# A decoder layer's start: modulation summed by one-column products, x transposed into SBUF, first loads in another order

## What is computed

```python
mod = silu(c) @ w_ada + b_ada                 # w_ada (1024, 3072)
shift, scale, gate = split(mod, 3)
h = x * rsqrt(mean(x*x) + eps) * norm_gain * (1 + scale) + shift
proj = h @ w_in                               # w_in (1024, 4808), split into u_a z_a q k v z_b q_idx k_idx w_idx g_a g_b
y_a = pooling(u_a) * silu(z_a)
y_b = sparse_attention(q, k, v, top 256 keys by the index scores of q_idx, k_idx, w_idx) * silu(z_b)
out = x + gate * ((sigmoid(g_a) * (y_a @ w_branch_a) + sigmoid(g_b) * (y_b @ w_branch_b)) @ w_out)
```

## Time and profile before

| | us |
|---|---|
| median of 3 runs | 896.79 |
| lowest, highest | 895.34, 902.83 |
| span of the profiled execution (first to last instruction) | 892.1 |

### The profile page before, as it was taken

The page is one execution under the profiler, slowest core; times in us unless marked ns, Lnnn a source line. Parts: engine busy times, 40 slices in busy tenths (PEclk is TensorE's granted clock), DMA queues, the critical chain, the costliest instruction groups (busy, mean ns, idle before and its releaser), DMA issues.

```text
span 892.1 us, 13967 instructions
## 1 busy us (share of the span) xinstructions
PE 805.7 (90%) x4991; PEld 710.8 (80%) x4994; DVE 623.8 (70%) x1238; ACT 338.3 (38%) x602; POOL 358.0 (40%) x301
## 2 busy tenths in 40 slices
PE   0349999998999999999999878899999999989998
PEld 0348999988988888887788756688888787869998
DVE  6974022787878898898888845577778895774542
ACT  4525322365562122223232112566667662320100
POOL 6414462055632577862652211654423002781110
PEclk9999999999999999999999979999999999999999
DMA  9811121113211331231123311633312005946432
GB/s 346 287 40 38 48 70 36 38 51 104 84 48 48 95 95 48 94 105 37 47 84 96 104 45 61 204 105 107 107 48 72 12 2 157 330 137 205 140 96 72
DMA packets 65200, 87.96 MB, mean 99 GB/s; under 512 B 5706, under 2 KB 44142, under 8 KB 65136
## 3 DMA queue, kind: packets, MB, share of 16 engines
q1 hardware_dynamic: 35116, 38.86, 14.2%
q10 hardware_dynamic: 28100, 41.96, 14.0%
q0 software_dynamic: 1920, 6.29, 1.9%
HBM read 66.12 MB, written 20.97 MB: 98 GB/s over the span
## 4 chain that ended last, share of the span: by engine, by line
PE 49%; DVE 35%; issue 5%; DVEq 5%; ACT 4%; DMA 1%; ACTq 0%; SPq 0%
DVE junk L1677 19%; PE pp L504 11%; PE pp L506 11%; PE pp L505 11%; PE pp L794 3%; PE ps L623 3%; PE ps L622 3%; PE pt L777 3%; DVE accept L1689 3%; DVE ada_acc L1520 2%; DVE cand L1691 2%; DVEq L1793 1%; PE pt L805 1%; DVE pT L1740 1%; DVE m_raw L1808 1%
## 5 line engine op out<-in xcount | busy, mean ns | idle before, releaser
L461 POOL TENSOR_TENSOR w_lo<-w_raw,w_hi 128x1024 fp32r<-128x1024 f32 (+1 forms) x54 | 131.9, 2461 | 201.4 <-ACT w_hi L450 201.1
L1677 DVE TENSOR_SCALAR_CACHE_REDUCE junk<-score,cand 128x384 uint8<-128x384 f32 (+1 forms) x186 | 168.6, 944 | 19.3 <-issue 13.3
L504 PE MATMUL pp<-hT_hi,w_hi 128*128 128x512 f32 x384 | 151.2, 394 | 0.0
L506 PE MATMUL pp<-hT_hi,w_lo 128*128 128x512 f32 x384 | 150.3, 391 | 0.0
L505 PE MATMUL pp<-hT_lo,w_hi 128*128 128x512 f32 x384 | 150.2, 391 | 0.0
L504 PE MATMUL pp<-w_hi,hT_hi 128*128 128x256 f32 (+1 forms) x416 | 119.2, 286 | 0.6 <-POOL hT_lo L1282 0.6
L506 PE MATMUL pp<-w_hi,hT_lo 128*128 128x256 f32 (+1 forms) x416 | 117.4, 282 | 0.0
L505 PE MATMUL pp<-w_lo,hT_hi 128*128 128x256 f32 (+1 forms) x416 | 117.3, 282 | 0.0
L504 PEld LDWEIGHTS pp<-hT_hi,w_hi 128*128 128x128 f32 x384 | 72.7, 189 | 16.1 <-issue 0.8
L506 PEld LDWEIGHTS pp<-hT_hi,w_lo 128*128 128x128 f32 x384 | 72.5, 189 | 15.3
L505 PEld LDWEIGHTS pp<-hT_lo,w_hi 128*128 128x128 f32 x384 | 72.6, 189 | 14.9
(11 more groups left out here) (246 smaller groups left out, 1737.1 us busy)
## 6 DMA issues: line engine op xcount, KB each, us to landing
w_raw<-in_w_in SPq DMA_DIRECT2D x36, 512.0 KB, 3.7
ada_w<-in_w_ada SPq DMA_DIRECT2D x8, 1024.0 KB, 14.4
sgb_spill<-stage ACTq DMA_DIRECT2D x16, 256.0 KB, 2.0
sga_spill<-stage ACTq DMA_DIRECT2D x16, 256.0 KB, 2.0
stage<-sga_spill ACTq DMA_DIRECT2D x16, 256.0 KB, 2.7
ma_spill<-stage POOLq DMA_DIRECT2D x16, 256.0 KB, 2.4
e_in<-sgb_spill ACTq DMA_DIRECT2D x16, 256.0 KB, 5.0
e_in<-ma_spill ACTq DMA_DIRECT2D x16, 256.0 KB, 6.4
```

The source lines that it names most:

```text
L461: nc.gpsimd.tensor_tensor(w_lo[:, ci % 2, 4 * p:4 * p + 4, 0:width], w_raw[:, n % RAW, :, 0:width], w_hi[:, ci % 2, 4 * p:4 * p + 4, 0:wid ...
L504: nc.tensor.matmul(o, a_hi, b_hi, start=first, stop=False)
L506: return nc.tensor.matmul(o, a_lo, b_hi, start=False, stop=last)
L1677: v.tensor_scalar(junk[:, n % 2, 0:keys(b)], score[:, score_at(b):score_at(b + 1)], least, None, ALU.is_ge, ALU.add, accum_out=cnt[:, n:n ...
```

## The change

- w_ada is loaded as seven row blocks ada_w[:, k, 0:2048] (1 MB, 8 KB per partition) for k = 0..6, then weight piece 0, then block 7 in two halves, piece 1, x tiles 0 and 1, piece 2 (which waits for the first w_lo), x tiles 2 and 3, wg_raw, the other pieces.
- The modulation is made on TensorE: for k = 1, 3, 5, 6, 7 (ADA_PE) 16 one-column products ada_w[:, k, ch]^T times c_silu[:, k], each into a column of its own in PSUM. k = 0, 2, 4 (ADA_V) are weighted and summed on VectorE in three 2048-column steps (ada_acc), then 16 products against ones. VectorE reduces the 6 x 16 columns. GpSimd does nothing for it.
- The transposes of half 1 are copied from PSUM to a new SBUF tile xT and stand between the column products in TensorE's program; h is made in place in xT once the modulation is known.
- Tiles 0 and 1 are made together, k by k, in both PSUM banks. hT_lo of half 1 is VectorE's for k in HT_V, GpSimd's for 5 and 7.
- GpSimd splits both pieces of chunk 0 as before; ScalarE's second hi split now comes after hT_hi of k = 1. Squares, root, scaling and transposes of half 0 move behind tiles 0 to 4 and 5 to 7 (H_AFTER), and `ps_value` counts one use of ps for the modulation instead of four.

```diff
-        return ps_at[key] + 4
+        return ps_at[key] + 1
-            lambda s: alloc(s, "ada_w", [P, 4, KD, HALF]),
+            lambda s: alloc(s, "ada_w", [P, KD, 2 * D]),
-            return alloc(s, "x_in", [P, NT, D]), alloc(s, "ada_acc", [P, 4, HALF])
+            return (alloc(s, "x_in", [P, NT, D]), alloc(s, "xT", [P, KD, HALF]), alloc(s, "ada_acc", [P, 2 * D]))
+        ADA_PE, ADA_V = [1, 3, 5, 6, KD - 1], [0, 2, 4]
+        ADA_COLS = 2 * D // P
+        HT_V, HT_P = [0, 1, 2, 3, 4, 6], [5, 7]
...
@@ sync @@
-            for i in range(4):
-                for j in range(2):
-                    ks = slice(j * KD // 2, (j + 1) * KD // 2)
-                    sp.dma_start(ada_w[:, i, ks], ada[:, ks, i * HALF:(i + 1) * HALF]).then_inc(ada_in[2 * i + j], 16)
-            for t in range(NT // 2):
-                sp.dma_start(x_in[:, t, :], x[t * P:(t + 1) * P, :]).then_inc(x_tile_in[t], 16)
+            for k in range(KD - 1):
+                sp.dma_start(ada_w[:, k, :], ada[:, k, 0:2 * D]).then_inc(ada_in[k], 16)
+            load_piece(0)
+            sp.dma_start(ada_w[:, KD - 1, 0:D], ada[:, KD - 1, 0:D]).then_inc(ada_in[KD - 1], 16)
+            sp.dma_start(ada_w[:, KD - 1, D:2 * D], ada[:, KD - 1, D:2 * D]).then_inc(ada_end, 16)
+            load_piece(1)
+            load_x(0)
+            load_x(1)
+            load_piece(2)
+            load_x(2)
+            load_x(3)
...
-        H_AFTER = {n: KD + 2 * (n - 1) for n in range(1, 5)}
+        H_AFTER = {5: [KD, KD + 1], 6: [KD + 2, KD + 3, KD + 4], 7: [KD + 5, KD + 6, KD + 7]}
@@ tensor @@
+            modulation = ps_claim("ada")
+            def ada_columns(i, first=0, end=ADA_COLS):
+                k = ADA_PE[i] if i < len(ADA_PE) else None
+                for j in range(first, end):
+                    ch, to = slice(j * P, (j + 1) * P), modulation[:, i * ADA_COLS + j:i * ADA_COLS + j + 1]
+                    if k is None:
+                        nc.tensor.matmul(to, ada_acc[:, ch], ones[:, 0:1], start=True, stop=True)
+                    else:
+                        last = nc.tensor.matmul(to, ada_w[:, k, ch], c_silu[:, k:k + 1], start=True, stop=True)
+                return last if k is not None else None
+            pe.wait_ge(c_silu_done, 1)
+            for i in range(2):
+                pe.wait_ge(ada_in[ADA_PE[i]], 16)
+                ada_columns(i)
             for n in range(2):
                 h_transposes(n)
...
+            pe.wait_ge(ada_in[ADA_PE[2]], 16)
+            ada_columns(2)
+            for n in range(2, 5):
+                h_transposes(n)
+            pe.wait_ge(ada_in[ADA_PE[3]], 16)
+            ada_columns(3)
+            for n in range(5, KD):
+                h_transposes(n)
+            pe.wait_ge(ada_sum, 1)
+            ada_columns(len(ADA_PE))
+            pe.wait_ge(ada_in[KD - 1], 16)
+            ada_columns(4, 0, ADA_COLS // 2)
+            pe.wait_ge(ada_end, 16)
+            ada_columns(4, ADA_COLS // 2).then_inc(ps_full, 1)
...
+            early = [pp_claim(("qi", i, t)) for i, t in QI_ORDER[:2]]
+            for k in range(KD):
+                if k % 4 == 0:
+                    pe.wait_ge(w_lo_done, k // 4 + 1)
+                pe.wait_ge(hT_hi_done, k + 1)
...
+                for o, (i, t) in zip(early, QI_ORDER):
+                    last = rows_step(o, t, name_of[("qi", i)], k, CW)
+                    if k == KD - 1:
+                        last.then_inc(pp_full, 1)
...
                 if n == NT:
                     pe.wait_ge(hT_hi_done, 2 * KD)
-                    pe.wait_ge(hT_lo_v, KD)
-                    pe.wait_ge(hT_lo_p, KD)
+                    pe.wait_ge(hT_lo_v, len(HT_V) + KD // 2)
+                    pe.wait_ge(hT_lo_p, len(HT_P) + KD // 2)
...
@@ scalar @@
             nc.scalar.activation(trig[:], reduced[:], ACT.Sin).then_inc(trig_done, 1)
-            square_half(0)
-            split_chunk_hi(act, 0)
+            split_piece_hi(act, 0)
...
             for n in range(KD):
                 ht_hi(n)
                 if n == 1:
-                    sqrt_half(0)
-            split_chunk_hi(act, 1)
-            scale_half(0)
+                    split_piece_hi(act, 1)
+            square(0)
...
+                if n == 0:
+                    split_piece_hi(act, 2)
+                    square(1)
+                if n == 1:
+                    square(2)
+                    split_piece_hi(act, 3)
+                if n == 2:
+                    square(3)
+                    sqrt_half(0)
+                if n == 3:
+                    act.wait_ge(dve_ready, V_RSQRT[0])
+                    scale(0)
+                    scale(1)
+                if n == 4:
+                    scale(2)
+                    scale(3)
+                for m in H_AFTER.get(n, []):
+                    ht_hi(m)
@@ gpsimd @@
-            split_chunk_lo(pool, 0)
-            for n in range(1, KD, 2):
+            split_piece_lo(pool, 0)
+            split_piece_lo(pool, 1)
+            for n in HT_P:
                 ht_lo(n)
...
@@ vector @@
+            ada_product(0)
+            ada_product(1)
             mean_half(1)
             rsqrt_half(1)
-            for i in range(1, 4):
-                ada_products(i)
+            ada_product(2)
+            v.tensor_scalar(col[:, 12 + KD:28], col[:, 12 + KD:28], 1.0, None, ALU.add)
+            for n in range(KD):
+                dve.wait_ge(pt_full, pt_at[("h", n)] + 1)
+                v.tensor_copy(xT[:, n, :], pt[pt_at[("h", n)] % 2][:]).then_inc(pt_free_v, 1)
+            parts = len(ADA_PE) + 1
+            dve.wait_ge(ps_full, 1)
+            v.tensor_reduce(shift[:], ps[0][:, 0:parts * ADA_COLS].rearrange("p (i j) -> p j i", i=parts), AX.X,
+                            ALU.add).then_inc(ps_free_v, 1)
...
+            for k in range(KD):
+                v.tensor_scalar(xT[:, k, :], xT[:, k, :], gmul[:, k:k + 1], shift[:, k:k + 1],
+                                ALU.mult, ALU.add).then_inc(h_raw_done, 1)
+                if k - 1 in HT_V:
+                    ht_lo(k - 1)
+            mean_half(0)
+            rsqrt_half(0)
+            for n in range(KD, 2 * KD + 2):
```

More of the change, by code:

```diff
@@ L362, in hybrid_layer @@
         x_tile_in = [sem(f"x_tile_in{t}") for t in range(NT)]
-        ada_in = [sem(f"ada_in{i}") for i in range(8)]
+        ada_in = [sem(f"ada_in{k}") for k in range(KD)]
+        ada_end = sem("ada_end")
         raw_in = [sem(f"raw_in{i}") for i in range(RAW)]
@@ L445, in split_chunk_hi @@
                 act.wait_ge(pp_full, chunk_done(ci - 2))
-            for n, (cj, p) in enumerate(pieces):
+            for n, (cj, _) in enumerate(pieces):
                 if cj == ci:
[L448 to L451, removed]
+                    split_piece_hi(act, n)
         def split_chunk_lo(pool, ci):
@@ L456, in split_chunk_lo @@
                 return
-            for n, (cj, p) in enumerate(pieces):
+            for n, (cj, _) in enumerate(pieces):
                 if cj == ci:
[L459 to L463, removed]
+                    split_piece_lo(pool, n)
         SCALED = {b: {3: 2 * n, 6: 2 * n + 1} if n < 2 else {1: 2 + n} for n, b in enumerate(range(FREE_BLOCKS, NT))}
@@ L852, in _, with square @@
             nc.scalar.activation(c_silu[:], c_col[:], ACT.Silu).then_inc(c_silu_done, 1)
[L854 to L858, removed]
+            def square(t):
+                act.wait_ge(x_tile_in[t], 16)
+                nc.scalar.activation(ps[1][:], x_in[:, t, :], ACT.Square, accum_out=ssx[:, t:t + 1]).then_inc(ssx_done, 1)
+                act.drain()
             def sqrt_half(f):
@@ L877, in ht_hi @@
                 act.wait_ge(h_raw_done, n + 1)
-                nc.scalar.activation(hT_hi[:, k, f * HALF:(f + 1) * HALF], h_raw[:, n % 4, :],
+                nc.scalar.activation(hT_hi[:, k, f * HALF:(f + 1) * HALF], xT[:, k, :] if f else h_raw[:, n % 4, :],
                                      ACT.Copy).then_inc(hT_hi_done, 1)
@@ L1551, in ht_lo @@
                 dve.wait_ge(hT_hi_done, j + 1)
-                v.tensor_tensor(hT_lo[:, k, tok], h_raw[:, j % 4, :], hT_hi[:, k, tok].bitcast(F32),
+                v.tensor_tensor(hT_lo[:, k, tok], xT[:, k, :] if f else h_raw[:, j % 4, :], hT_hi[:, k, tok].bitcast(F32),
                                 ALU.subtract).then_inc(hT_lo_v, 1)
-            for n in range(2 * KD + 2):
-                if n == 2:
-                    mean_half(0)
-                if n == 4:
-                    rsqrt_half(0)
-                if n == KD:
-                    ht_lo(n - 2)
+            for k in range(KD):
[6 more added lines that the diff above has]
+            for n in range(KD, 2 * KD + 2):
                 if n < 2 * KD:
@@ L1572, in _ @@
                     dve.sem_inc(pt_free_v, 1)
-                if n >= 2 and n % 2 == 0 and n != KD:
+                if n >= KD + 2 and n % 2 == 0:
                     ht_lo(n - 2)
```

121 lines of the change are left out of this document (55 added, 66 removed).

## The result

| | before | after |
|---|---|---|
| median of 10 runs, us | 896.42 (895.25 to 902.83) | 906.82 (903.82 to 1041.49) |
| span of the profiled execution | 892.1 | 906.2 |

The ratio is 1.0103, with a 95% interval of 1.0068 to 1.0138: 1% slower, 10.4 us between the medians. One run after, 1041.49 us, fell in a slow state of the chip (mean granted clock 0.77, 0.97 to 0.99 in the others) and is left out of the ratio; the other nine have a median of 906.18, 9.8 above before. The forecast was 909.3, with a range of its own from 904 to 913; the line above which it called the kernel slower, 905.8, is passed by 1.0 us (by 0.4 with the nine).

A forecast was written before the change was run, and what follows sets the result against it. TensorE's column products were taken to bound the first h: 10.3 us late there, 5.1 won by the pair, 7.3 lost to stalls, 12.5 in all, so 909.3 us. Range 891.0 to 913.5, the likeliest's own 904 to 913.

The forecast's parts named there:

- x scaled: Start of the kernel: VectorE's earlier statistics and ScalarE's four scalings have x ready at 26.3 us, before at 32.3.
- The column products decide: Modulation on TensorE: 96 written one-column products at 0.43 us, 41.1 us in all, put first h 10.3 us later.
- The landing: DMA at the start: w_ada blocks arrive at 2.7 us a MiB, the last at 32.5 us, long before the products end.
- The end of the products: TensorE before h: column products and 32 transposes, with 0.5 us of bank waits, end at 62.7 us.
- The clock rival: Rival, chance 0.2: TensorE's clock rises early during transposes and column products, tile 8 comes 4.5 us early, 892.3 us.
- Pair: First h to tiles 0 and 1 done: 13.7 us instead of 18.8, so 5.1 us won.
- Stalls between pair and tile 8: TensorE waits from the pair's end to tile 8: this stretch takes 29.4 us, 7.3 more than before.
- The clock rises: Rival, chance 0.2: written products on TensorE go at 0.23 us before h, giving 892.3 us.
- The late half of x costs nothing: Rival, chance 0.12: ScalarE's squares and splits fit between copies after the pair, 7.3 us fall away, 902.0 us.
- h is held longer: Rival, chance 0.08: GpSimd's lo parts overlap VectorE's h steps, each k takes 2 instead of 1.27 us, 915 us.
- The sum: Whole start: 10.3 us late at h, 5.1 won, 7.3 lost, 12.5 us in all, giving 909.3 us.
- The span forecast: Profiled execution as a whole: span goes from 892.1 to 904.6 us.

The follow-up runs named there:

- e4: Changed kernel with 128 moving columns instead of 1 in each modulation product: 893.6 us, ratio 0.996 to the kernel before.
- e1: Changed kernel with VectorE summing blocks 0 to 6 and TensorE making only block 7 and the sum over partitions: 902.7 us, ratio 1.005 to the kernel before.
- e2: Changed kernel with ScalarE's and GpSimd's work for x's other half and weight splits ahead of h, its transposes after tiles 2 to 5: 896.4 us, ratio 0.997.
- e8: Changed kernel with tile 1 made after tile 0 instead of paired with it: 910.1 us, ratio 1.013 to the kernel before.
- e3: Changed kernel with ScalarE's hi split of weight piece 1 moved ahead of the hT_hi loop: 912.4 us, ratio 1.016 to the kernel before.
- e6: e4 and e2 together on the changed kernel, last sum's and k = 7's columns swapped so nothing read is overwritten: 884.6 us, ratio 0.985.
- e9: e6 with ScalarE making h's hi parts before late splits and scaling, GpSimd h's lo parts first: 880.4 us, ratio 0.980 to the kernel before.

## Why the prediction came out right

| step | forecast | measured after |
|---|---|---|
| x scaled | 26.3 | 25.3 |
| a block of 16 written products | 6.85 | 6.83, once 3.88 |
| column products end | 62.7 | 59.4 |
| first h | 63.5 | 60.2 |
| first h to pair done | 13.7 | 12.9 |
| pair done to start of tile 8 | 29.4 | 29.7 |
| start of tile 8 | 106.6 | 102.8 |
| tile 8 late | 12.5 | 10.9 |

*The column products decide: right.* They run from 14.48 on, 192 recorded, with transposes between and no wait for a landing, and VectorE idles for them. The landing was off the path, as forecast: the first weight piece released its split at 28.36 (forecast 29.8). e4 shows it as a cause: it changes the width of these products alone, and the mark moves by 14.7. e1, which takes four of the six blocks off TensorE and reorders the rest, moves it by 9.0.

*The end of the products, 62.7: mis-sized by 3 us.* The clock rose for one block after 12 transposes, which I had priced only as a rival that holds throughout. e2 and e8 are without the rise, and there the reduction comes at 62.35 and 62.39 and h at 63.2. The sum was right for the case that it described; that the case comes and goes from one profiled execution to another was not in it. The clock rival's break-even of 0.27 us a written product holds with the transposes at 0.194; at the rival's own 0.11 it is 0.30. Nothing rests on it.

*Pair: nearly right for its size, only in part for its reason.* The h step beside GpSimd's w_lo took 2.59 us instead of 0.54 (2.05 more, for 2.4), and e3 takes 2.0 us off the pair by moving it (70.98 - 60.11 = 10.9 for 12.9). The other steps went at 1.06 us a k where 1.27 was forecast. The forecast had 5.1 us won against before, here it is 5.9 (12.9 for 18.8). e8 gives 4.0 of it to the pairing; the other 1.9 would be the root and transposes that are no longer between the h steps, which no run took apart. The Trainium skill (GPSIMD Engine Reference, Key points) names two-port modes and two SBUF inputs of VectorE as what is in contention with GpSimd. The step with one SBUF input was held for GpSimd's whole instruction (2.59 us by 2.46), which fits the page only if this step runs in a two-port mode; no row shows the mode. VectorE's copies out of PSUM took 0.69 throughout, two of the eight (29.25, 30.11) beside GpSimd's w_lo.

*Stalls between pair and tile 8: right.* TensorE waits 1.07 us for w_lo before tile 4 (forecast 1.8), 1.5 at the transposes (2.5) and 4.77 before tile 8 (4.0), and e2 removes them all. The sum missed one thing behind them: in the idle time the clock falls, and tile 8's products go at 0.21 instead of 0.12 us apart, about 2.2 us over 24 of them. In e2, without the idle time, the clock stays up.

*The rivals.* "The clock rises" was false as a state that holds, and true for 3.4 us; had it held, e4 says that h comes at 45.4 and the time at 893.6, for which I had 46.5 and 892.3. The Trainium skill has both rules in TensorE: Matmul & The Clock Gate: recent busyness sets the clock ("What's actually happening"), and transposes do not count the same way (Part 4). The runs agree with neither plainly. 14 us of one-column products without a gap did not lift the clock, and 32 of them did not keep it up once it had risen (49.4 to 52.8); e4's eight transposes at 1.04 us run at the higher clock, between wide products. "The late half of x costs nothing" was false: 9.6 us by e2. "h is held longer" was false: but for the step beside w_lo and the last (1.43), ScalarE's hi parts follow each other by 1.06 us (65.78 to 68.95 are three steps).

*The sum.* Against the forecast, h came 3.3 earlier, the pair took 0.8 less, the stalls 0.3 more and tile 8 some 2.2 more: 12.5 - 1.6 = 10.9 late at tile 8, as measured, and 10.4 between the medians. The forecast time is 2.5 too high: 2.1 of it are this (12.5 for 10.4), 0.4 that the median of three runs before (896.8) lay above that of ten. Two misses of 3.3 and 2.2 us, nearly all of both from TensorE's clock, thus partly cancelled. That the total came so near is partly luck: had the clock not risen at 49.4, as in e2 and e8, tile 8 would have been some 14 us late. The span forecast, 904.6, was 1.6 too low: the profiled execution after has the two stretches at half the clock far behind, worth 3.5 us, that the sum had not. To carry the difference over to the median was right: of the 4.7 us between span and median only 1.7 lie around the span (907.9 for 906.2 in the profiled execution after, and as much in the other runs), the other 3 were how far the profiled execution before lay under the median.

## What to carry to other kernels

Work moved to an engine that is idle at that moment is not free if it stands on the path: price it at the clock that this work itself will get, and if its products are narrow, try wider ones: here 128 columns instead of one took a block from 6.83 to 3.74 us. Where h, or whatever releases the dense stretch, comes earlier, look on every engine's queue for what stands ahead of the next step: here 9.6 us lay in work that had been put behind the stretch and 5 more in work put in front of it (e6 against e9). Compare kernels at a mark ahead of any part that varies from run to run.

## What was not expected of the hardware

- One-column f32 products, back to back for 14 us (14.48 to 28.2), stay at 0.333 us per weight load. With 128 moving columns the loads go to 0.192 and a block from 6.83 to 3.74 us.
- After 12 transposes and some 3 one-column products the clock rose (49.4) and fell again (52.8) while one-column products ran without a gap. With the same instructions there it rose in e3 and not in e2 and e8.
- In 4.8 us without work on TensorE (98.0 to 102.8) its granted clock fell, at 100.6, and it stayed at 0.50 until 107.4, through 4.6 us of work.
- A 128x512 VectorE step in SBUF took 2.59 us beside a GpSimd subtraction, and 0.54 without.
- Six-element VectorE steps in the bisection, the same code, take 0.751 us on the mean in the profiled execution of the kernel after and 0.854 in that of e3; with the two steps beside it this makes 7 us of a kernel's time.
